# Paged attention of the sample group: V pages issued from GpSimd's queue instead of SyncE's

## The reference, cut to what matters

```python
past_k = cache_sb_k[b][page_table]          # pages of 128 tokens x 12 heads x 64, float32
past_v = cache_sb_v[b][page_table]
mix_s = sb_sample(qs, ks, vs, sb_bias[b], past_k, past_v)

z = einsum('bqhd,bkhd->bhqk', q, k) * 64 ** -0.5 + bias
log_keep = where(mask, log_sigmoid(-z), 0)
log_after = cumsum(log_keep, axis=3, reverse=True) - log_keep
a = where(mask, exp(log_sigmoid(z) + log_after), 0)
out = einsum('bhqk,bkhd->bqhd', a, v)
```

## Time and profile before

| | |
|---|---|
| median of 3 runs | 3349.26 us (3347.88 to 3355.92) |
| the profiled execution | 3354.68 us, of which the span of instructions is 3352.8 us |
| busy share of the span | PE 94%, PEld 82%, DVE 55%, ACT 31%, POOL 3% |
| sample attention | from about 2129.4 to 2396.9 us of the span |
| DMAs of that stage | 128 K pages and 128 V pages of 384 KB, all from SP |
| DMA engines in the 40 slices | busy 9 tenths or more in two slices only, both of this stage |

### The profile page before, as it was taken

How to read it: one execution, slowest core, us unless ns; L and a number is a source line. 1 busy time by engine, 2 the same in 40 slices (tenths; PEclk the granted TensorE clock), 3 DMA queues, 4 the chain that set the end, 5 groups by cost and what they waited for, 6 DMA issues and landing times.

```text
span 3352.8 us, 52573 instructions
## 1 busy us (share of the span) xinstructions
PE 3136.9 (94%) x20072; PEld 2764.9 (82%) x20072; DVE 1853.9 (55%) x2826; ACT 1043.9 (31%) x1673; POOL 92.5 (3%) x161
## 2 busy tenths in 40 slices
PE   6996899999999998999869989999999999999997
PEld 6994799999999997899645655656799999999996
DVE  4126235676666667410347877655425666667666
ACT  5224133222222224321324443445323222222221
POOL 0010000000000000000000000000000000000000
PEclk8998899999999999999968887999999999999998
DMA  4122201111111111132320010599611111111111
GB/s 139 39 96 73 74 26 51 38 38 44 50 38 38 56 38 32 62 103 91 120 90 19 19 38 6 193 383 397 243 35 33 55 38 38 56 38 38 40 42 65
DMA packets 188124, 260.38 MB, mean 78 GB/s; under 512 B 9560, under 2 KB 138222, under 8 KB 188044
## 3 DMA queue, kind: packets, MB, share of 16 engines
q1 hardware_dynamic: 170752, 197.23, 17.1%
q0 software_dynamic: 16512, 61.71, 5.7%
q10 hardware_dynamic: 780, 0.34, 0.0%
HBM read 238.24 MB, written 27.68 MB: 79 GB/s over the span
## 4 chain that ended last, share of the span: by engine, by line
PE 83%; DVE 6%; DMA 4%; ACT 3%; issue 3%; SPq 2%; ACTq 0%; POOL 0%; DVEq 0%; POOLq 0%
PE ps L319 22%; PE ps L320 22%; PE ps L321 22%; PE ps L909 4%; PE ps L935 3%; PE ps L428 2%; DMA pv_tail<-in_cache_sb_v_dram 2%; PE ps L922 2%; DVE x L1886 1%; PE ps L1141 1%; PE ps L1180 1%; SPq L1082 1%; PE ps L1158 1%; PE ps L1678 1%; ACT prob L1509 1%
## 5 line engine op out<-in xcount | busy, mean ns | idle before, releaser
L1886 DVE TENSOR_TENSOR x<-x,ps 128x512 f32<-128x512 f32 (+1 forms) x792 | 538.9, 688 | 305.4 <-PE ps L321 304.5
L319 PE MATMUL ps<-act_hi,w_hi 128*128 128x370 f32 x2112 | 701.6, 332 | 1.4 <-DVE act_lo L463 1.4
L320 PE MATMUL ps<-act_lo,w_hi 128*128 128x370 f32 x2112 | 700.7, 332 | 0.0
L321 PE MATMUL ps<-act_hi,w_lo 128*128 128x370 f32 x2112 | 698.9, 331 | 0.0
L319 PE MATMUL ps<-w_hi,act_hi 128*128 128x256 f32 (+1 forms) x1800 | 507.2, 282 | 5.1 <-DVE w_lo L315 2.5
L320 PE MATMUL ps<-w_lo,act_hi 128*128 128x256 f32 (+1 forms) x1800 | 506.7, 281 | 0.0
L321 PE MATMUL ps<-w_hi,act_lo 128*128 128x256 f32 (+1 forms) x1800 | 505.2, 281 | 0.0
L319 PEld LDWEIGHTS ps<-act_hi,w_hi 128*128 128x128 f32 x2112 | 398.1, 188 | 5.7 <-DVE act_lo L463 1.7
L320 PEld LDWEIGHTS ps<-act_lo,w_hi 128*128 128x128 f32 x2112 | 398.0, 188 | 2.0
L321 PEld LDWEIGHTS ps<-act_hi,w_lo 128*128 128x128 f32 x2112 | 397.4, 188 | 0.0
L315 DVE TENSOR_TENSOR w_lo<-w_raw,w_hi 128x2048 fp32r<-128x2048 f32 x73 | 167.4, 2293 | 353.5 <-ACT w_hi L311 353.5
(11 more groups left out here) (286 smaller groups left out, 3920.4 us busy)
## 6 DMA issues: line engine op xcount, KB each, us to landing
w_raw<-in_w_up_dram SPq DMA_DIRECT2D x88, 512.0 KB, 4.7
pk_w<-in_cache_sb_k_dram SPq DMA_DIRECT2D x64, 384.0 KB, 5.2
pv_w<-in_cache_sb_v_dram SPq DMA_DIRECT2D x64, 384.0 KB, 5.2
pk_tail<-in_cache_sb_k_dram SPq DMA_DIRECT2D x64, 384.0 KB, 5.3
pv_tail<-in_cache_sb_v_dram SPq DMA_DIRECT2D x64, 384.0 KB, 5.3
d_raw<-in_w_down_dram POOLq DMA_DIRECT2D x44, 512.0 KB, 3.6
projected<-stage POOLq DMA_DIRECT2D x13, 1024.0 KB, 5.2
w_raw<-in_w_in_b_dram SPq DMA_DIRECT2D x20, 512.0 KB, 4.3
```

What stands on the lines that cost most here:

```text
L319: pe.matmul(out, ahi, bhi, start=first, stop=False, **kw)
L320: pe.matmul(out, ahi, blo, start=False, stop=False, **kw)
L321: return pe.matmul(out, alo, bhi, start=False, stop=last, **kw)
L1886: dve.tensor_tensor(xs, xs, ps[0:ROWS[t], DN_BANK[(2 * t + c) % 4], :], ALU.add).then_inc(dn_ev, 1)
```

## The change

The V pages' loads leave SP's program and become a program of their own on POOL, `pool_bs`, which runs after `pool_bp`. It has its own `value_load` of the page numbers and its own waits: `bs_set` (the page table is there), `w_ok` (the buffer of `pv_w` is free), `bp_lo` (the prompt attention is done) before V of group 1, and `bs_av` before V of group g+2. SP keeps the K pages and the new tokens' values; the wait on `bs_av` that stood ahead of the V pages is kept on SP once for each batch, ahead of `new_values`. The V pages of group 0 of the first batch were issued ahead of the prompt attention by SP; POOL issues them after the last load of `pool_bp`. Sizes, buffers, semaphores and the four computing programs stay as they are.

```diff
@@ sp_bs
-            def values(b, g, page):
-                for j in range(2):
-                    sp.dma_start(pv(g)[:, j, :],
-                                 A["cache_sb_v"][0, bass.ds(page[j], 1)].rearrange("a t h d -> t (a h d)")).then_inc(bs_v[g % 2], 16)
...
                         sp.wait_ge(bs_tr, b * (3 * NGR) + (3 * g + 3))
                         keys(*after(b, g, 4), page)
-                    if g + 2 < NGR or not last_batch:
-                        page = pages(*after(b, g, 2))
-
-                        sp.wait_ge(bs_av, b * NGR + (g + 1))
-                        values(*after(b, g, 2), page)
                     if g == 0 and not last_batch:
+                        sp.wait_ge(bs_av, b * NGR + 1)
                         new_values(b + 1)
...
             for g in range(2):
                 keys(0, g, pages(0, g))
-            values(0, 0, pages(0, 0))
-            page = [pages(0, g) for g in (1, 2, 3)]
+            page = [pages(0, g) for g in (2, 3)]
 
             sp.wait_ge(bp_lo, 2 + 4 * NPAIR)
             for g in (2, 3):
-                keys(0, g, page[g - 1])
-            values(0, 1, page[0])
+                keys(0, g, page[g - 2])
             new_values(0)
             batches(sp, batch)
+
+        def pool_bs(pool):
+            pool.wait_ge(bs_set, 16)
+
+            def pages(b, g):
+                return [pool.value_load(page_t[0:1, bass.ds(b * PAGES + (PAGES - 2 - 2 * g + j), 1)]) for j in range(2)]
+
+            def values(b, g, page):
+                for j in range(2):
+                    pool.dma_start(pv(g)[:, j, :],
+                                   A["cache_sb_v"][0, bass.ds(page[j], 1)].rearrange("a t h d -> t (a h d)")).then_inc(bs_v[g % 2], 16)
+
+            def batch(b, first_batch, last_batch):
+                for g in range(NGR):
+                    if g + 2 < NGR or not last_batch:
+                        page = pages(*after(b, g, 2))
+
+                        pool.wait_ge(bs_av, b * NGR + (g + 1))
+                        values(*after(b, g, 2), page)
+
+            pool.wait_ge(w_ok, out0[1] + 1)
+            values(0, 0, pages(0, 0))
+            page = pages(0, 1)
+            pool.wait_ge(bp_lo, 2 + 4 * NPAIR)
+            values(0, 1, page)
+            batches(pool, batch)
@@ block.gpsimd
                     pool_bp(pool)
+                    pool_bs(pool)
                     pool.wait_ge(bs_lo, NB)
```

## The result

The changed kernel takes 3376.24 us in the median of five runs (3364.65 to 3378.3) against 3349.26 us before (3345.68 to 3355.92, five runs): a ratio of 1.0072, 95% interval 1.0052 to 1.0093. By the ratio it is slower by about 24 us, by the two medians by 27.0 us, where 7 us less had been forecast. The profiled execution has a span of 3376.8 us.

The account below looks back on a forecast made before the run. SP's single file of issues was taken to make V pages late in part of each batch. 9.7 us of DMA waits - 1.25 (last V pages) - 1.6 (to DVE) = 6.9 us less: 3349.26 to 3342.4 us, range 3337 to 3355.

Parts of the forecast that it names:

- the kept wait on SP: SP's wait on `bs_av` once a batch, K pages of group 5 and later queued behind it; costed at nothing.
- the V loop: From end of `use(g)` to V(g+2) landed: 6.7 to 6.9 us available, 5.0 to 6.5 taken, so V in time.
- SP's wake-up: Time from end of `use` to the first V issue: 0.16 us, read from SP and taken for POOL.
- the ceiling of 9.7 us: Most the change could gain: PE's waits for V pages, 9.3 us, and for K pages, 0.4 us.
- SP's single file of issues: In the sample attention, SP's issuing, 3.58 us a group without slack, ends last in part of each batch.
- that lead: K's four buffers: three groups, 12 us, lie ahead of a late K pair, so its delay stays hidden.
- The bounds: Limits for V's second page landing after `use`: 5.0 us from below, 7.4 us (0.70 + 4.3 + 2.4) from above.
- DVE's product: PE's wait for it returns where V waits vanish: 10 x 0.16 = 1.6 us, from 4.3 to about 6 us.
- The slower one: Rival: V lands later from POOL, 7.4 us after `use`; 15.5 us more, 3364.8 us; chance 0.15.
- its point of decision: Landing time after `use` from which the rival of later V from POOL decides: 6.9 us.
- The one that says the engines are the bound: Rival: the DMA engines are full, so nothing is gained; 3349 to 3351 us; chance 0.25.
- the row with 179 GB/s: Stretch with both queues loading, engines busy 1.02, short rows of other data; cited for the rival of later V from POOL.

Follow-up runs that it names:

- Experiment 14: Changed kernel with new values after group 3 and V pages from ACT's queue, those of group 0 behind ACT's copies for the batch: 3362.59 us, ratio 1.0054.
- experiment 1: Changed kernel with the new tokens' values and their kept wait issued by SP after group 3 of a batch instead of group 0: 3367.25 us, ratio 1.0048.
- experiment 4: Changed kernel with the queues swapped: K pages from POOL, V pages and new values from SP: 3376.55 us, ratio 1.0064.
- Experiment 12: Changed kernel with new values after group 3, and POOL's two page reads moved behind its wait on use(g): 3394.85 us, ratio 1.0120.
- experiment 6: Kernel before, everything from SP, with only the first half of each K row loaded: 3340.31 us, ratio 0.9977.
- 13: Changed kernel with new values after group 3 and V pages issued from ACT's queue instead of POOL's: 3377.97 us, ratio 1.0067.
- 2: Changed kernel with K pages of group g+4 issued by SP after use(g-1), when V pages go out: 3395.75 us, ratio 1.0125.
- 8: Kernel before with only the new tokens' values issued from POOL, all pages still from SP: 3344.07 us, ratio 0.9990.
- 11: Kernel before with only the new tokens' values from POOL, measured again in five rounds: 3346.92 us, ratio 0.9991.

## Why the prediction was wrong

Two terms of the sum failed: the kept wait on SP, put at nothing, and the V loop, of which the text said "Then V is in time", with SP's wake-up for POOL and no K page beside V. The size of the first is shown; the second is shown to fail, and how it divides is open.

By V waits of PE, the way from before to after goes 9.3 (one queue), 17.3 (two queues, prompt start), 24.1 (V from POOL), 31.6 us (with the kept wait after group 0). The three steps are 8.0, 6.8 and 7.5 us, 22.3 in all, of the stage's 25.3 us. Another 3.3 us is a single stand of PE in the last batch ("issue" above), and other waits give back 3.1 us: 22.3 + 3.3 - 3.1 = 22.5. The remaining 2.8 us are PE's own work, busy 246.71 us before and 249.53 us after; after long waits part of it ran at a granted clock of 0.50 (last section). The steps come from different kernels and need not add exactly.

The third step, the kept wait, is shown by one edit. How the rest divides between the two queues and POOL's late start is not. Experiment 14's stage is 6.0 us shorter than experiment 1's, but 3.2 us of that are PE's busy time (246.87 and 243.67 us) and 2.9 us the stand; the 6.8 us of V waits came back as waits for ACT and DVE. In experiment 4 V started as promptly, and PE waited 33.3 us for it. Experiment 12 by proportion, 0.48 us of 0.81, would put some 14 us (by the times) to 19 us (by the stage) on the late start, an estimate that does not agree with 6.8 us. What stands is that both cost: two queues with a prompt start by the V waits of experiments 4 and 14, a later start by experiment 12.

**What bounds the kernel.** No run contradicts the ceiling of 9.7 us: even with half of K's bytes gone the stage of the kernel before was only 6.8 us shorter. That SP's single file of issues was the cause was half right at best. It stands in the chain, and in about a third of the pairs SP issued V 0.4 to 1.5 us after `use`; but halving K's bytes with the same issues removed 5.2 of the 9.3 us. The two were bound up: a busy queue and a busy issuer show the same wait.

**SP's part: the step that failed first.** The kept wait was costed at nothing, "hidden by that lead". The lead did hide it from K: PE waited for no K page. But the text asked only who waits for K. What is late next is V: the engines ran nearly empty at 120 to 154 GB/s, and the K pages held back came out in one burst in front of V. SP now reached the wait early, at about 2272.4, and stood there until 2281.4, where before the V waits of each group had kept K at a walk. The sum had it at nothing; experiment 1 prices it at 11.5 us of the stage, 7.5 of them V waits.

**POOL's part: the term that was mis-sized.** The 0.54 us an issue were right (0.537 us), a page read took about 0.39 us where 0.28 had been taken, and POOL's round had room for it. The wake-up was taken from SP, 0.16 us; POOL took 0.68. This term is in the V loop, and it had no row of POOL behind it. The bounds left it out: they were drawn for the landing only. The Trainium skill ("DMA: Bandwidth & Descriptors", Latency and other measured facts) gives about 1 us to the first byte of a DMA from GpSimd and about 0.6 us from SP or ACT. That is another stretch, from the DMA on and not from the wait to the DMA, and no run here shows a first byte by itself; it points the same way as the 0.5 us between the starts measured here.

**The V loop.** The chosen 5.0 to 6.5 us after `use` was wrong for the page that decides. Medians of landing mix the first page of a pair with the second and easy groups with hard ones; the page on the chain landed 8.4 us after `use`, beyond the upper bound of 7.4. "A V page no longer stands behind K pages issued before it" was the reasoning that failed: pages issued at the same time or later now stand beside it, and the landing on the chain took 7.14 us, against 6.7 us at the upper bound (4.3 + 2.4).

**DVE's product.** Forecast to grow from 4.3 to about 6 us; it fell to 3.4 us, while V waits, which lie over it, grew. With V waits down to 4.1 us, in experiment 6, it was 4.6 us, so hardly more than the 4.3 before: the 1.6 us that the sum gave it were too much.

**The rivals.** The slower one named the right mechanism (V later from POOL, K's share of the engines) and its point of decision, 6.9 us after `use`; it was given 0.15 and priced at 15.5 us, without the gap and with SP's wake-up. The stage grew by 25.3. The one that says the engines are the bound is refuted for the changed kernel by their share, 0.94 over 2150 to 2380 with 366 GB/s where the same window before has 1.01 and 391, and by 430 GB/s in loaded windows; the row with 179 GB/s was no precedent for page loads. For the kernel before it was right in part: there fewer bytes took 5.2 us of V waits away. The Trainium skill's rule ("DMA: Bandwidth & Descriptors", Issuing engines are not separate DMA queues), that a second issuer saves only the sequencer's time, allows a small gain or none, and there was none. It names no cost, and there was one: PE waited 8.0 us more for V in experiment 14, with both queues prompt, and the time was 1.0054 of before.

## What to carry to other kernels

A single queue is also a schedule: it says which transfer the engines serve first. Before taking a stream out of it, ask for the transfer that is due soonest what will now run beside it, and price its loop from the end of use to the landing of the second page, with the new issuer's own wake-up. A wait that is harmless to the stream behind it can still harm another one, by first starving and then flooding the engines they share.

## What the runs showed of the hardware

- POOL started a V pair 0.66 to 0.68 us after the `use` that it waited for; SP (experiment 4) and ACT (experiments 13 and 14) took 0.17 to 0.2 us nearly always. A pair takes 1.13 us from POOL and 0.85 us from SP. A page read takes 0.28 us on SP and about 0.39 us on POOL.
- A page of 128 rows of 3072 bytes goes out from POOL in 80 packets and from SP in 144.
- With both queues at work the engines moved up to 430 GB/s at a share of 1.07, no less than the 418 GB/s from SP's queue alone.
- In the last batch, which is code of its own, PE stood for 3.3 us ahead of `use(0)`, 6.8 us after that batch's first scores, with nothing in the profile to wait for, and then ran at half clock for some microseconds:

```profile
2388.00:2390.00 2.00, 2.00 (x18) 0.65 (x18) 0.00 (x0) 0.00 (x0) 0.20 (x1) 0.50 0.21 83
2390.00:2392.00 2.00, 2.00 (x15) 1.19 (x10) 0.00 (x0) 0.95 (x3) 0.88 (x2) 0.50 0.49 121
```

The granted clock is 0.50 here, the 1.2 GHz level, after a window in which PE did nothing (2384 to 2386 us). The stand was 3.1 us in experiment 1, 2.3 in 2, 1.4 in 4 and 0.2 in 14, and is absent before and in 6, 8, 11 and 13. Its cause stays open.
- A long wait for V did the same to the clock. After this one it is 0.50 from 2189 to 2192 us, and 12 matmuls take 1.93 us instead of 1.06:

```profile
2189.35 1.93 PE L1195 MATMUL ps<-pv_tail,at_t 128*32 128x256 f32 x12 [2.95 <-DMA pv_tail<-in_cache_sb_v_dram]
```
